# Windowed attention by head pairs in 24 substeps, with row- and column-half matmuls

## The reference, cut to what matters

```python
q = rms_norm(q.reshape(B, S, 16, 64), q_norm_g)       # 16 query heads, 4 key heads
k = rms_norm(k.reshape(B, S, 4, 64), k_norm_g)
q, k = rotary(q, ...), rotary(k, ...)
# blocks of 128 queries; each sees its own and the two neighbouring key blocks
s = einsum('bnqhgd,bnjhd->bhgnqj', qb, kwin) * 64 ** -0.5    # masked beyond +-128
m = maximum(max(s, -1), sink)
p = exp(s - m); p = p / (sum(p, -1) + exp(sink - m))
o = einsum('bhgnqj,bnjhd->bnqhgd', p, vwin)
return o * silu(gate)
```

## Time and profile before

| what | value |
|---|---|
| median of 3 executions | 3257.03 us (3250.7 to 3257.6) |
| profiled execution | 3256.87 us, span 3254.9 us |
| TensorE matmul busy | 3155.0 us (97%) |
| VectorE busy | 1720.7 us (53%) |
| GpSimd busy | 1325.8 us (41%) |
| ScalarE busy | 1148.9 us (35%) |
| TensorE granted clock, mean | 0.986 of full |

### The profile page before, as it was taken

One profiled execution on the slowest core, in us unless ns is written; L12 is line 12 of the kernel. 1 busy time (PEld: TensorE's weight loads), 2 busy tenths in 40 slices (PEclk: granted clock), 3 DMA queues, 4 the chain that ended last, 5 costly groups with the idle time before them and its releaser, 6 DMA issues.

```text
span 3254.9 us, 41274 instructions
## 1 busy us (share of the span) xinstructions
PE 3155.0 (97%) x13924; PEld 2496.6 (77%) x13924; DVE 1720.7 (53%) x2561; ACT 1148.9 (35%) x1649; POOL 1325.8 (41%) x966
## 2 busy tenths in 40 slices
PE   7999999999999999999999999998999999999998
PEld 5877776767888787777776788887788887788886
DVE  7965576465442497575556545247764252531114
ACT  3232333355242223332234543324554332332223
POOL 4433433411555443443432135453334444354543
PEclk9999999999999999999999999999999999999999
DMA  3222222201322322222221022331222323232222
GB/s 133 95 67 71 87 74 71 71 27 31 120 96 97 119 97 78 78 77 65 84 76 48 27 91 91 100 105 60 69 67 83 105 85 100 68 103 97 97 97 84
DMA packets 73405, 267.83 MB, mean 82 GB/s; under 512 B 8144, under 2 KB 9168, under 8 KB 72912
## 3 DMA queue, kind: packets, MB, share of 16 engines
q1 hardware_dynamic: 70560, 254.84, 23.7%
q10 hardware_dynamic: 2736, 11.53, 1.0%
HBM read 262.14 MB, written 4.19 MB: 82 GB/s over the span
## 4 chain that ended last, share of the span: by engine, by line
issue 46%; PE 27%; POOL 24%; DVE 3%; DVEq 1%; POOLq 0%; ACT 0%; ACTq 0%
POOL wlo L274 24%; PE gem L302 7%; PE gem L304 7%; PE gem L303 7%; PE gem L649 1%; PE gem L651 1%; PE gem L650 1%; PE xp L658 1%; DVE U L1767 1%; DVE zlo L1292 0%; DVEq L1788 0%; PE xp L732 0%; POOLq L271 0%; DVE hlo L1292 0%; PE gem L326 0%
## 5 line engine op out<-in xcount | busy, mean ns | idle before, releaser
L274 POOL TENSOR_TENSOR wlo<-raw,whi 128x512 fp32r<-128x512 f32 x956 | 1325.0, 1407 | 1895.9 <-ACT whi L805 1895.2
L302 PE MATMUL gem<-hhi,whi 128*128 128x512 f32 x2352 | 947.1, 403 | 0.0
L304 PE MATMUL gem<-hhi,wlo 128*128 128x512 f32 x2352 | 916.8, 390 | 0.0
L303 PE MATMUL gem<-hlo,whi 128*128 128x512 f32 x2352 | 915.7, 389 | 0.0
L805 ACT ACTIVATE whi<-raw 128x1024 fp32r<-128x1024 f32 x478 | 504.1, 1055 | 603.0 <-PE gem L304 498.7
L303 PEld LDWEIGHTS gem<-hlo,whi 128*128 128x128 f32 x2352 | 442.1, 188 | 105.5 <-issue 16.5
L302 PEld LDWEIGHTS gem<-hhi,whi 128*128 128x128 f32 x2352 | 441.9, 188 | 105.2 <-issue 16.5
L304 PEld LDWEIGHTS gem<-hhi,wlo 128*128 128x128 f32 x2352 | 441.6, 188 | 93.3
L302 PE MATMUL gem<-zhi,whi 128*128 128x512 f32 x960 | 378.6, 394 | 12.4 <-DVE zlo L1491 9.5
L304 PE MATMUL gem<-zhi,wlo 128*128 128x512 f32 x960 | 376.1, 392 | 0.0
L303 PE MATMUL gem<-zlo,whi 128*128 128x512 f32 x960 | 376.0, 392 | 0.0
(11 more groups left out here) (257 smaller groups left out, 3538.3 us busy)
## 6 DMA issues: line engine op xcount, KB each, us to landing
raw<-in_slabs SPq DMA_DIRECT2D x478, 512.0 KB, 3.3
U<-in_x SPq DMA_DIRECT2D x4, 512.0 KB, 7.5
U<-in_x ACTq DMA_DIRECT2D x1, 2048.0 KB, 8.8
xsave<-U ACTq DMA_DIRECT2D x1, 2048.0 KB, 6.4
U<-xsave ACTq DMA_DIRECT2D x1, 2048.0 KB, 7.8
out_y<-yr SPq DMA_DIRECT2D x8, 256.0 KB, 2.1
tab<-in_tab_ret ACTq DMA_DIRECT2D x2, 512.0 KB, 7.9
tab<-in_tab_att ACTq DMA_DIRECT2D x2, 512.0 KB, 3.7
```

Of the source, the lines that this page charges most:

```text
L274: part = pool.tensor_tensor(wlo[:, k % 4, c], raw[:, k % 2, c], whi[:, k % 4, c].bitcast(f32), O.subtract)
L302: pe.matmul(o, wh, hi, start=(n == 0), stop=False)
L303: pe.matmul(o, wh, lo, start=False, stop=False)
L304: mm = pe.matmul(o, wl, hi, start=False, stop=(n == len(terms) - 1))
```

## The change

Heads go in pairs p (0 to 7), three substeps t per pair, 24 in all: c = t % 3 picks the query blocks (0 and 3; 1; 2) of both heads of the pair. Scores of the two heads alternate between the partition halves, block by block; the output matmuls alternate between the output halves. Two sets of score banks alternate with t. The gate uses bank 3 of `gem` alone: ScalarE writes tanh(x/2) of it, VectorE makes (tanh + 1) * x and by that frees the bank, and `head_out` brings in the factor 0.5. GpSimd multiplies the probabilities of c = 1 and 2 by their reciprocal. The keys' norms move into the last `ret_out` group. Then the edits at the start, in `ln_shifted` and in the reads behind the second layer norm.

On TensorE:

```diff
+                half(G + 2, 0, u + 2, (z_ready, L * 40 + 12 + PRIMED))
+                a_norm(0)
+                half(G + 2, 1, u + 2)
+                a_turn(0)
+                a_norm(1)
+                half(G + 2, 2, u + 2)
+                a_turn(1)
+                half(G + 2, 3, u + 2)
...
                     for k in range(1, 8):
                         hslab(G, k, u)
-                    a_turn(k - 1)
-                    a_norm(k)
+                    if k > 1:
+                        a_turn(k)
+                    a_norm(k + 1)
...
-                            pe.wait_ge(evac[bank], u + (2 + j % 4 // 2) + PRIMED)
+                            pe.wait_ge(evac[3], u + 2 + j + PRIMED)
...
+                    for n, cols in spans(c):
+                        for hf in range(2):
+                            rows = slice(hf * 64, hf * 64 + 64)
+                            mm = pe.matmul(scores_of(t, hf)[:, cols], QR[p][rows, n * P:(n + 1) * P],
+                                           KA[rows, pr, lo * P:hi * P], start=True, stop=True)
+                    mm.then_inc(s_done, 1)
...
+                    if c == 0 and p:
+                        pe.wait_ge(ao_read, L * 8 + p)
+                    pe.wait_ge(t_ready, L * 48 + t * 2 + 2)
+                            for hf in range(2):
+                                d = slice(hf * 64, hf * 64 + 64)
+                                mm = pe.matmul(xp[d, 3, n * P:(n + 1) * P],
+                                               VTA[:, j, pr * P + hf * 64:pr * P + hf * 64 + 64], PT[hf][:, at:at + P],
+                                               start=(j == lo), stop=(j == hi - 1))
...
+                for t in range(24):
+                    p, c = t // 3, t % 3
+                    if t >= 3:
+                        turn_p(t - 3)
+                    gate_rows(p * NT + (0, 3, 6)[c], p * NT + (0, 5, 8)[c])
+                    qk(t)
+                    if t == 0:
+                        a_turn(8)
+                        a_norm(9)
+                    elif t == 1:
+                        a_turn(9)
+                    if t >= 3:
+                        a_pv(t - 3)
+                    gate_rows(p * NT + (0, 5, 8)[c], p * NT + (3, 6, 8)[c])
```

On ScalarE:

```diff
+                for t in range(26):
+                    if t >= 3:
+                        turned_p(t - 3)
+                    if t < 24:
+                        exps(t)
+                    if t == 0:
+                        a_inv(9)
+                    if t % 3 == 1 and t < 24:
+                        high(G, 8 + t // 3 + 3)
+                    if t == 1:
+                        act.preload_act_table_set("exp_and_others")
+                    if t % 3 == 2 and t < 24:
+                        act.wait_ge(slab_done, G * 4 + (8 + t // 3 + 1) + PRIMED)
+                        act.activation(TH, gem[:, 3, :], A.Tanh, scale=0.5).then_inc(th_ready, 1)
```

On VectorE (the third part places the key tiles between the parts of `add_out`, the last is in `ln_shifted`):

```diff
+                def gate(p):
+                    dve.wait_ge(th_ready, L * 8 + (p + 1))
+                    stt(SG[:, p % 4, :], TH, 1.0, gem[:, 3, :], O.add, O.mult).then_inc(evac[3], 1)
+                for t in range(24):
+                    maxes(t)
+                    if t == 0:
+                        a_norm_rope(8)
+                    elif t == 1:
+                        a_norm_rope(9)
+                    if t:
+                        normalise(t - 1)
+                    if t % 3 == 0 and t:
+                        gate(t // 3 - 1)
+                    if t % 3 == 2 and t > 2:
+                        head_out(t // 3 - 1)
...
+                for k in range(4):
+                    add_out(G + 2, u + 2, (k,))
+                    if k in (1, 2):
+                        a_norm_rope(k - 1)
...
                 shift(1)
-                shift(2)
-                shift(3)
```

On GpSimd:

```diff
+            def probabilities(L, t):
+                c = t % 3
+                pool.wait_ge(r_ready, L * 16 + t // 3 * 2 + c)
+                for hf in range(2):
+                    last = pool.tensor_scalar(PB[c][hf], PB[c][hf], REC[c][:, hf:hf + 1], None, O.mult)
+                last.then_inc(p_ready1, 1)
...
+                for p in range(9):
+                    if p:
+                        probabilities(L, 3 * p - 1)
+                    if p < 8:
+                        low((first + p) // 4, (first + p) % 4)
+                        probabilities(L, 3 * p + 1)
```

On ScalarE, behind the second layer norm, and at the start:

```diff
-            for i in range(2, 5):
-                affine(2, i, XC[:, i, :], B_LN1)
+            affine(2, 2, XC[:, 2, :], B_LN1)
             act.wait_ge(slab_done, Gp * 4 + 2 + PRIMED)
...
-                if i == 3:
-                    high(0, 1, False)
-            high(0, 2, False)
+            high(0, 1, False)
```

More of the change, by code:

```diff
@@ L276, in low, with lows @@
                 part.then_inc(lo_done, 1)
[L278 to L282, removed]
+            def probabilities(L, t):
[4 more added lines that the diff above has]
+                last.then_inc(p_ready1, 1)
+            def lows(a, b):
+                while a % 4 and a < b:
+                    low(a // 4, a % 4)
+                    a += 1
+                if a // 4 < b // 4:
+                    with pool.Fori(a // 4, b // 4) as G:
+                        for k in range(4):
+                            low(G, k)
+                for n in range(max(a, b // 4 * 4), b):
+                    low(n // 4, n % 4)
+            at = 0
+            for L in range(DEPTH):
+                first = (L * LAYER_GROUPS + ATT[0]) * 4 + 11
+                lows(at, first)
+                for p in range(9):
[4 more added lines that the diff above has]
+                        probabilities(L, 3 * p + 1)
+                at = first + 8
+            lows(at, N_SLABS)
         @block.tensor
@@ L966, in layer @@
                         .then_inc(vt_ready, 1)
-                for k in range(4):
-                    high(G + 2, k + 3)
                 def a_inv(n):
@@ L1239, in _ @@
                 read(j, PL[:, 4 + j, :], A.Copy)
-            for i in range(5, NT):
+            for i in range(3, NT):
                 affine(2, i, XC[:, i, :], B_LN1)
@@ L1491, in gated, with add_out @@
                             tt(zlo[:, w, :], OT[:, w, :], zhi[:, w, :].bitcast(f32), O.subtract).then_inc(z_ready, 1)
-                def add_out(G, u):
-                    for k in range(4):
+                def add_out(G, u, ks=range(4)):
+                    for k in ks:
                         product(G, k)
@@ L1607, in layer @@
-                for s in range(16):
-                    maxes(s)
-                    if s == 0:
-                        a_norm_rope(7)
-                    elif s == 1:
-                        a_norm_rope(8)
-                        a_norm_rope(9)
-                    else:
-                        head_out(s - 2)
-                    normalise(s)
-                head_out(14)
-                head_out(15)
+                dve.wait_ge(evac[0], u + 2 + PRIMED)
+                dve.wait_ge(evac[1], u + 2 + PRIMED)
@@ new lines, in normalise @@
+                def normalise(t):
+                    c, i = t % 3, t % 2
+                    w = 2 * len(BLOCK_SETS[c])
+                    dve.wait_ge(p_exp, L * 24 + (t + 1))
+                    tt(DEN[:, 0:w], RSUM[i][:, 0:w], ES[i][:, 0:w], O.add)
+                    dve.drain()
+                    rec = dve.reciprocal(REC[c][:, 0:w], DEN[:, 0:w])
+                    if c:
+                        rec.then_inc(r_ready, 1)
+                        return
+                    dve.drain()
+                    for hf in range(2):
+                        for b, (n, cols) in enumerate(spans(0)):
+                            x = PB[0][hf][:, cols]
+                            last = ts(x, x, REC[0][:, hf * 2 + b:hf * 2 + b + 1], None, O.mult)
+                    last.then_inc(p_ready0, 1)
@@ L1619, in layer @@
+                dve.drain()
+                head_out(7)
                 dve.drain()
```

290 lines of the change are left out of this document (126 added, 164 removed).

## The result

| | before | after |
|---|---|---|
| median of four executions, us | 3256.35 (3250.70 to 3257.60) | 3282.47 (3274.27 to 3283.11) |
| profiled execution: span, us | 3254.9 | 3281.3 |
| mean granted clock of TensorE | 0.986 | 0.976 |

The ratio is 1.0078, with a 95% interval of 1.0058 to 1.0098. The changed kernel is slower, by 26 us. The main case of the prediction said 3284.

What follows compares the result with a forecast made beforehand. TensorE, busy 97%, was taken as the bound, with its saved work returning as waits. From 3257 us, -21 attention, +13 key norms, -8 small edits, +16 contention, +20 and +7 clock gave 3284; range 3238 to 3312.

Steps and rivals of the forecast that it cites:

- main case: For the whole kernel: gate wait, contention and some clock falls, 3284 us, own range 3260 to 3306, chance 0.53.
- TensorE's own work, 13.9 us a pair: Per head pair in the attention loop: overlapping array halves cut TensorE's work to 13.9 us, 3.6 less than 17.48.
- the slots that stand alone: First and last instruction of scores or output lack overlap: c = 1 scores fall from 1.41 to 1.06 us.
- The chain of 7.6 us: VectorE's list from a pair's last scores to its gate product takes 7.6 us; a pair lasts 17.7 against 17.48.
- Contention, +16: GpSimd's split and multiply slow VectorE's chain at two meetings, taken as 1.0 us per pair, 16 times: +16 us.
- The clock, +27: Idle stretches lower TensorE's clock: half the pairs at 2.5 us, +20; three falls at key norms and loop starts, +7.
- The start of the attention: In each layer, from first scores to the end of `qk(5)`, waits included: 33.5 us.
- Key norms, +13: Before each layer's first scores, two waits of 2.3 us plus two more matmuls: +6.5 per layer, +13 us.
- Changeover and small edits: Per layer the 7.9 us bank changeover goes; edits at start, in `ln_shifted` and behind the second norm give -8 us.
- -21: Attention of both layers, 155.3 against 166.0 us each, mostly from the bank changeover going: -21 us.
- the 7 us set aside for further falls: Three clock falls from eight new stalls of 2.3 to 3.2 us at key norms and loop starts: +7 us.
- clock up, little contention: Whole kernel: clock stays up and GpSimd disturbs little, 3248 us, between 3238 and 3260, chance 0.24.

## Why the prediction held, point by point

**TensorE's own work, 13.9 us a pair.** Right. Starts in the timeline of the changed kernel give output 0.81 us (c = 1, 2) for the predicted 0.82, and the pair of 14.82 us contains 1.0 us of waits. The reason that I gave for the slots that stand alone was wrong for the scores: those of c = 1 take 713.67 - 712.82 = 0.85 us, not 1.06, and the order of the heads does not matter to them. The Trainium skill's page "TensorEngine Tiling (Array Packing)", Key Properties, says that tiles operate independently; the trace agrees, with two heads' scores 0.01 us apart in either order.

**The chain of 7.6 us.** Right in sum and in place, by errors that cancel within it. The scores of substep 3p+2 end at 717.41 + 0.92 = 718.33 us and the gate row starts at 725.96: 7.63 us. In it `maxes` of c = 2 takes 2.09 us for 1.7, since its first small operation lies beside the split; the seven other terms come to 0.36 us less than I had. The pair without a fall of the clock is 17.41 us for the predicted 17.7, with waits of 2.04 and 1.19 us at the two places named, for 1.9 and 1.5.

**Contention, +16.** Mis-sized. The 7.63 us already contain the one meeting that there is, 0.73 instead of 0.17 us; nothing is to be added to them. The multiply that the change puts on GpSimd costs nothing that shows, by the run without it: 3 us within the noise, and none of it in the attention. The page "GPSIMD Engine Reference" of the Trainium skill, Specifications, has the two engines share an interface where VectorE has two SBUF inputs. For `head_out`'s subtraction beside the multiply the trace does not show that cost on VectorE: it takes 0.69 us, as undisturbed, and the multiply stretches, two of them from 2.46 to 2.88 us.

**The clock, +27.** Right in kind. Between the ends of `qk(5)` (700.94) and `qk(23)` (814.01) the changed kernel needs 113.1 us for six pairs, 18.8 each; with the waits filled it is 104.4, 17.4 each. That is 8.7 us, and 10.2 in layer 2 (114.9 and 104.7): 19 in both, where I had 20. I had put it on half of the pairs at 2.5 us; in layer 1 four of five pairs in a row are 1.3 to 2.8 us longer than the undisturbed one. The rest of what filling gave lies at the loop's end (in layer 1 18.6 against 16.5 us behind `qk(23)`), which the prediction had at 15.6.

**The start of the attention.** Mis-sized, low: 33.5 us up to the end of `qk(5)` in the prediction, 700.94 - 661.91 = 39.0 measured. The two waits in it are as foreseen (3.05 and 2.54 us for 3.2 and 2.8), but the granted clock of that stretch is 0.83, and the first output waits 2.55 us for its copies.

**Key norms, +13.** Mis-sized, low. The two waits per layer are 3.09 and not 2.3 us, because of the product beside the slab split, and the clock stands at 0.76 behind the first. First scores come 10.2 us later in layer 1, though the start gained 26.83 - 25.08 = 1.8; that makes 12 us for 6.5. In layer 2 the stage grows by 15.5 us. The run with the norms sooner divides these 27.5 us: 24 go with the place in VectorE's list, 12.4 of them as waits and about 12 as lower clock behind them, and the rest is the two matmuls a layer.

**Changeover and small edits.** The changeover's wait is gone as predicted; the small edits are worth 9.1 us alone, for 8.

**The sum.** The forecast of 3284 against 3282.5 owes its closeness to luck: single stages were off by 3 to 15 us. By stages of the profile the attention costs +10 us, for -21 + 16 + 20 = +15 forecast (+22 with the 7 us set aside for further falls); the key norms +27.5, for +13; the small edits and what else lies behind the second attention -11, for -8. Contention that did not come and key norms that cost twice their price made up for each other. The rival "clock up, little contention" (3248) had half of its condition: the contention was little, the clock did not stay up. Filled waits made the pairs of that case, with the clock still down at the start and the key norms, and it ran at 3260.

**What stays open.** The longer wait of a pair is enough to bring the clock down in every second pair (the run with `gate` sooner); no run kept the gate's wait and removed the longer one, so what the gate's wait does alone is not shown. Why GpSimd's split slows VectorE's operations while its multiply does not slow the subtraction was not taken apart, and no run moved the split away from them.

## What to carry to other kernels

Time saved on the bounding engine is only saved if every chain of the other engines between two of its instructions gets shorter too; add up those chains in the order of their lists, and then try the lists in another order before giving the change up. Here the change lost 26 us, and the same instructions in another order won 63, 9 of them by the small edits. A wait of 2 to 3 us on TensorE cost its own length and often the lower clock behind it: judge a change by where it leaves TensorE idle, not only by how long; and an engine's small operation that releases a third engine is not small.

## What the runs showed of the hardware beyond the expected

Two heads' matmuls in different row halves ran side by side even when four instructions of one half stood ahead of the other's in the program (start 0.01 us apart). For column halves in that order the overlap was partial: 1.55 us for 16 instructions, 1.09 when alternating. By the price of before, 0.117 us each, they would have been 1.87. Counted from start to start, 12 of them take 1.07 us in that order, 0.81 alternating, and 1.40 by the price of before.

Work that nobody needs made the kernel faster: 112 matmuls in TensorE's waits, 21 us less, granted clock of the pairs from 0.89 to 1.00.

GpSimd's split of a slab that started with a 128x512 product of VectorE took that product from 0.75 to 1.79 us, and was itself 2.93 instead of 2.51. A 128x2 operation that began late in a split ended with it, 0.73 us long instead of 0.17; beside GpSimd's multiply it stayed at 0.16.
